# A third fast pair in the output projection, and T sums rounded and split in one instruction each

## The reference

```
h = x + token_mixing(rmsnorm(x, norm_mix), ...)      # 4 mixers, gates, merged @ w_out
h = h + peer_ffn(rmsnorm(h, norm_ffn), wq, subkeys, u, v)

# end of token_mixing
merged = sum over 4 branches of sigmoid(z @ gate_up[i]) * (o_i @ w_branch_i)
return merged @ w_out                                # 4096 x 4096: the output projection

# peer_ffn: queries, top-k keys, act = gelu(xn @ u.T), a sparse coefficient matrix, then
return wmat @ v                                      # 4096 x 4096: the last stage
```

## Time and profile before

| | us |
|---|---|
| median of three runs | 1894.08 |
| the profiled execution's own time | 1893.71 |
| its span, first to last instruction | 1891.9 |
| TensorE busy (8855 matmuls) | 1887.2 |
| VectorE busy | 1477.8 |
| ScalarE busy | 979.1 |
| GpSimd busy | 72.1 |

### The profile page before, as it was taken

The page is one execution under the profiler, slowest core; times in us unless marked ns, Lnnn a source line. Parts: engine busy times, 40 slices in busy tenths (PEclk is TensorE's granted clock), DMA queues, the critical chain, the costliest instruction groups (busy, mean ns, idle before and its releaser), DMA issues.

```text
span 1891.9 us, 25741 instructions
## 1 busy us (share of the span) xinstructions
PE 1887.2 (100%) x8855; PEld 1560.3 (82%) x8855; DVE 1477.8 (78%) x2159; ACT 979.1 (52%) x1195; POOL 72.1 (4%) x109
## 2 busy tenths in 40 slices
PE   9999999999999999999999999999999999999999
PEld 8888878888888888888888888888888888888887
DVE  7578875685567889989765555899989978999897
ACT  7654644445466556546454464444444455555553
POOL 0010020210100000000000000000000000000000
PEclk9999999999999999999999999999999999999999
DMA  9976667767675569867887776767766678666664
GB/s 325 349 226 167 184 196 239 202 179 237 204 235 173 183 196 298 270 227 235 260 262 225 218 224 220 232 206 222 220 202 200 200 210 291 222 215 220 213 221 156
DMA packets 202384, 423.96 MB, mean 224 GB/s; under 512 B 46752, under 2 KB 125216, under 8 KB 201504
## 3 DMA queue, kind: packets, MB, share of 16 engines
q1 hardware_dynamic: 174048, 369.35, 62.9%
q0 software_dynamic: 7248, 27.92, 4.3%
q10 hardware_dynamic: 20976, 25.19, 3.9%
HBM read 395.79 MB, written 26.61 MB: 223 GB/s over the span
## 4 chain that ended last, share of the span: by engine, by line
PE 100%; DMA 0%; ACT 0%; DVE 0%; SPq 0%; issue 0%
PE acc L707 26%; PE acc L710 25%; PE acc L714 25%; PE acc L755 3%; PE acc L757 3%; PE acc L761 3%; PE acc L1193 2%; PE side L1072 1%; PE side L1071 1%; PE side L1073 1%; PE acc L1199 1%; PE acc L1113 1%; PE acc L1112 1%; PE acc L1118 1%; PE side L882 1%; PE side L999 1%
## 5 line engine op out<-in xcount | busy, mean ns | idle before, releaser
L1660 DVE TENSOR_TENSOR w_lo<-w_raw,w_hi 128x1024 fp32r<-128x1024 f32 (+1 forms) x649 | 784.9, 1213 | 367.6 <-ACT w_hi L1240 361.0
L1240 ACT ACTIVATE w_hi<-w_raw 128x1024 fp32r<-128x1024 f32 (+1 forms) x649 | 680.7, 1052 | 722.7 <-PE acc L714 585.7
L707 PE MATMUL acc<-w_hi,xt_hi 128*128 128x512 f32 x1348 | 366.4, 394 | 0.0
L710 PE MATMUL acc<-w_hi,xt_lo 128*128 128x512 f32 x1348 | 360.6, 389 | 0.0
L714 PE MATMUL acc<-w_lo,xt_hi 128*128 128x512 f32 x1348 | 360.5, 389 | 0.0
L710 PEld LDWEIGHTS acc<-w_hi,xt_lo 128*128 128x128 f32 x1348 | 253.1, 188 | 53.0
L707 PEld LDWEIGHTS acc<-w_hi,xt_hi 128*128 128x128 f32 x1348 | 251.3, 188 | 55.2 <-issue 4.9
L714 PEld LDWEIGHTS acc<-w_lo,xt_hi 128*128 128x128 f32 x1348 | 253.1, 188 | 52.8
L707 PE MATMUL acc<-w_hi,x_hi 128*128 128x512 f32 x640 | 173.5, 393 | 0.0
L710 PE MATMUL acc<-w_hi,x_lo 128*128 128x512 f32 x640 | 171.3, 390 | 0.0
L714 PE MATMUL acc<-w_lo,x_hi 128*128 128x512 f32 x640 | 171.2, 390 | 0.0
(11 more groups left out here) (387 smaller groups left out, 2076.0 us busy)
## 6 DMA issues: line engine op xcount, KB each, us to landing
w_raw<-in_stream SPq DMA_DIRECT2D x504, 512.0 KB, 4.2
w_raw<-in_w_in SPq DMA_DIRECT2D x16, 496.0 KB, 3.9
w_raw<-in_w_in SPq DMA_DIRECT2D x16, 480.0 KB, 5.2
w_raw<-in_w_in SPq DMA_DIRECT2D x16, 464.0 KB, 4.0
w_raw<-in_w_in SPq DMA_DIRECT2D x16, 448.0 KB, 4.2
w_raw<-in_w_in SPq DMA_DIRECT2D x16, 432.0 KB, 3.9
w_raw<-in_w_in SPq DMA_DIRECT2D x16, 416.0 KB, 4.6
w_raw<-in_w_in SPq DMA_DIRECT2D x16, 400.0 KB, 3.7
```

The costliest lines, as they stand in the source:

```text
L707: pe.matmul(o[h], lhs(k0 + j, h)[0], wh[j], start=first and j == 0, stop=False)
L710: pe.matmul(o[h], lhs(k0 + j, h)[1], wh[j], start=False, stop=False)
L1240: nc.scalar.activation(w_hi[:, slot, 0:width], w_raw[:, slot, 0:width], ACT.Copy).then_inc(hi_ready, 1)
L1660: nc.vector.tensor_tensor(w_lo[:, slot, 0:width], w_raw[:, slot, 0:width], w_hi[:, slot, 0:width].bitcast(F32), ALU.subtract).then_inc(lo_ ...
```

## The change

A third pair is put in the output projection, groups 4 and 5, with six fast k pairs (`FAST`); two plain groups are left. Pairs of the last stage are renumbered from 3. The T sums of a fast k pair are rounded by one ScalarE instruction of 2048 columns and split by one VectorE instruction of 2048 columns; TensorE waits for both halves ahead of its first T matmul. The third pair adds its side banks at the times of the long pairs (`late`) and has its own `out_sums`. The row work of groups 2 to 5 starts 14, 12, 16 and 8 chunks later. The loads of x for groups 4 and 5 wait until the last T of the output projection is used, those for groups 6 and 7 until the third pair's side banks are added; `h_hi` waits for the last T too, from group 2 on.

```diff
@@ -106,11 +106,12 @@
-OUT_PAIRS = (Pair(0, CH_OUT, FAST[4:], 0), Pair(1, CH_OUT + 2 * CPG, FAST, 2))
-V_PAIRS = (Pair(2, CH_V, FAST_LAST[5:], 8), Pair(3, CH_F, FAST_LAST, 10), Pair(4, CH_F + 2 * CPG, FAST_LAST, 17),
-           Pair(5, CH_F + 4 * CPG, FAST_LAST, 24))
-OUT_PLAIN = CH_OUT + 4 * CPG
-HEAD = {0: 2, 2: 4}
+OUT_PAIRS = (Pair(0, CH_OUT, FAST[4:], 0), Pair(1, CH_OUT + 2 * CPG, FAST, 2), Pair(2, CH_OUT + 4 * CPG, FAST, 8))
+OUT_T = 14
+V_PAIRS = (Pair(3, CH_V, FAST_LAST[5:], OUT_T), Pair(4, CH_F, FAST_LAST, 16), Pair(5, CH_F + 2 * CPG, FAST_LAST, 23),
+           Pair(6, CH_F + 4 * CPG, FAST_LAST, 30))
+OUT_PLAIN = CH_OUT + 6 * CPG
+HEAD = {0: 2, 3: 4}
@@ -417,7 +418,8 @@
     out_t_lo = at("out_t_lo", [P, 2, 2, 512], F32R, PJ0 + 8 * KB)
-    out_sums = [at(f"out_sums{i}", [P, 512], F32, MG0 + (8 + 2 * i) * KB) for i in range(2)]
+    out_sums = [[at(f"out_sums{n}{i}", [P, 512], F32, MG0 + (8 + 4 * (n // 2) + 2 * i) * KB) for i in range(2)]
+                for n in range(len(OUT_PAIRS))]
     t_tiles = {True: (out_t_raw, out_t_hi, out_t_lo), False: (t_raw, t_hi, t_lo)}
@@ -575,13 +577,13 @@
     GATE_OUT = {MIX_CH[b] + n * (1 + MIX_K[b] // 2) + LEAD: (b, n) for b in MERGE for n in range(GRP)}
-    OUT_OUT = {CH_OUT + (n + 1) * CPG + LEAD: n for n in range(4, GRP)}
+    OUT_OUT = {CH_OUT + (n + 1) * CPG + LEAD: n for n in range(6, GRP)}
     MIX_HI = {mix_end("a", n) + LEAD + 8: n for n in range(GRP)}
-    ROW_END = {n: CH_OUT + {0: 2 * CPG, 1: 2 * CPG + 20, 2: 4 * CPG, 3: 4 * CPG + 10}.get(n, (n + 1) * CPG)
+    ROW_END = {n: CH_OUT + {0: 2 * CPG, 1: 2 * CPG + 20, 2: 4 * CPG + 14, 3: 4 * CPG + 22, 4: 6 * CPG, 5: 6 * CPG + 8}.get(n, (n + 1) * CPG)
                for n in range(GRP)}
@@ -1077,8 +1079,8 @@
-                if pair.order > 2:
-                    pe.wait_ge(block_free, 4 * (pair.order - 3) + 2 * i + h + 1)
+                if pair.order > 3:
+                    pe.wait_ge(block_free, 4 * (pair.order - 4) + 2 * i + h + 1)
                 elif h == 0:
@@ -1093,9 +1095,9 @@
                     for d in range(2):
-                        pe.wait_ge(t_hi_done, 2 * n + d + 1)
-                        pe.wait_ge(t_lo_done, 2 * n + d + 1)
                         if d == 0:
+                            pe.wait_ge(t_hi_done, 2 * n + 2)
+                            pe.wait_ge(t_lo_done, 2 * n + 2)
                             thrice(side[:, 1, :], s_tile[0], t, 0, first, last)
@@ -1121,14 +1123,14 @@
                     pe.wait_ge(xt_lo_done, KT + kp + 1)
-                if pair.order == 2:
+                if pair.order == 3:
                     pe.wait_ge(wmat_lo, kp + 1)
-                if first and pair.order in (1, 3, 4, 5):
+                if first and pair.order in (1, 2, 4, 5, 6):
                     pe.wait_ge(pure_free, pair.order)
-                if first and pair.order == 2:
+                if first and pair.order == 3:
                     pe.wait_ge(gates_put, ROUNDS)
                 if first:
-                    pe.wait_ge(s_lo_done, 12 if pair.order >= 2 else 8)
+                    pe.wait_ge(s_lo_done, 12 if pair.order >= 3 else 8)
                 def to_c21():
...
@@ -1402,6 +1404,8 @@
                 act.wait_ge(row_moved, 16 * (n + 1))
+                if n >= 2:
+                    act.wait_ge(t_used, OUT_T)
                 if k >= NX2:
@@ -1599,9 +1603,9 @@
                     act.wait_ge(t_used, n)
-                for d in range(2):
-                    act.wait_ge(t_made, 2 * n + d + 1)
-                    nc.scalar.activation(flat(hi_tile[:, d]), flat(raw[:, d]), ACT.Copy).then_inc(t_hi_done, 1)
+                act.wait_ge(t_made, 2 * n + 2)
+                nc.scalar.activation(hi_tile[:].rearrange("p d j n -> p (d j n)"),
+                                     raw[:].rearrange("p d j n -> p (d j n)"), ACT.Copy).then_inc(t_hi_done, 2)
@@ -2352,9 +2356,9 @@
                     dve.wait_ge(t_lo_done, 2 * n)
-                if kp == pair.fast[0] and pair.order == 2:
+                if kp == pair.fast[0] and pair.order == 3:
                     dve.wait_ge(s_lo_done, 12)
-                if kp == pair.fast[0] and pair.order in (1, 3, 4, 5):
+                if kp == pair.fast[0] and pair.order in (1, 2, 4, 5, 6):
                     dve.wait_ge(pure_free, pair.order)
@@ -2370,10 +2374,9 @@
                 raw, hi_tile, lo_tile = t_tiles[pair in OUT_PAIRS]
-                for d in range(2):
-                    dve.wait_ge(t_hi_done, 2 * n + d + 1)
-                    nc.vector.tensor_tensor(flat(lo_tile[:, d]), flat(raw[:, d]), flat(hi_tile[:, d]).bitcast(F32),
-                                            ALU.subtract).then_inc(t_lo_done, 1)
+                dve.wait_ge(t_hi_done, 2 * n + 2)
+                low, raws, hi = (t[:].rearrange("p d j n -> p (d j n)") for t in (lo_tile, raw, hi_tile))
+                nc.vector.tensor_tensor(low, raws, hi.bitcast(F32), ALU.subtract).then_inc(t_lo_done, 2)
@@ -2386,16 +2389,16 @@
                     return rows[:, h, n * 512:(n + 1) * 512]
-                n = 2 * (pair.order - 2) + i
+                n = 2 * (pair.order - 3) + i
                 return h_rows[:, h, n * 512:(n + 1) * 512]
-                u, v = (t[:] for t in (out_sums if pair in OUT_PAIRS else sums))
+                u, v = (t[:] for t in (out_sums[pair.order] if pair in OUT_PAIRS else sums))
                 p1, p5, p6, p7 = (side[:, i, :] for i in range(4))
                     dve.wait_ge(t_used, pair.first_t + len(pair.fast))
-                    if pair.order == 2:
+                    if pair.order == 3:
                         dve.wait_ge(h_loaded, 64)
@@ -2438,7 +2441,8 @@
-                if pair.fast[-1] == 12:
+                late = pair.fast[-1] == 12 or pair.order == 2
+                if late:
                     for step, at in enumerate(((14, 1), (14, 1), (15, 0), (15, 1))):
@@ -2447,7 +2451,7 @@
                         t_sums(after, 0)
-                if kp in (13, 14) and pair.fast[-1] < 12:
+                if kp in (13, 14) and not late:
                     add_pure(pair, 2 * (kp - 13) + i)
@@ -2475,12 +2479,12 @@
                 if pair:
-                    pair_tasks(pair, kp, i, {0: OUT_PAIRS[1], 2: V_PAIRS[1]}.get(pair.order))
+                    pair_tasks(pair, kp, i, {0: OUT_PAIRS[1], 1: OUT_PAIRS[2], 3: V_PAIRS[1]}.get(pair.order))
                 between(s)
             for pair in V_PAIRS[1:]:
-                before = V_PAIRS[pair.order - 3]
-                after = V_PAIRS[pair.order - 1] if pair.order < 5 else None
+                before = V_PAIRS[pair.order - 4]
+                after = V_PAIRS[pair.order - 2] if pair.order < 6 else None
                 for kp in range(CPG):
@@ -2602,7 +2606,9 @@
                 if n == 4:
-                    pool.wait_ge(pure_free, 2)
+                    pool.wait_ge(t_used, OUT_T)
+                if n == 6:
+                    pool.wait_ge(pure_free, 3)
                 pool.dma_start(rows[:, :, n * 512:(n + 1) * 512], io["x"][:, :, n * 512:(n + 1) * 512])\
```

More of the change, by code:

```diff
@@ L516, in group_number @@
     def group_number(pair, i):
-        return GN_OUT + 2 * pair.order + i if pair in OUT_PAIRS else GN_V + 2 * (pair.order - 2) + i
+        return GN_OUT + 2 * pair.order + i if pair in OUT_PAIRS else GN_V + 2 * (pair.order - 3) + i
     def pair_bank(pair, i):
```

## The result

The changed kernel takes 1897.61 us (median of 20 runs, 1895.49 to 1900.47); the kernel before, run beside it on the same chip, 1894.26 us (20 runs, 1893.52 to 1896.23). The ratio is 1.0017, with a 95% interval of 1.0011 to 1.0023: 3.35 us slower, where the forecast of 1894.1 us meant no change to speak of, and 0.8 us outside the range. The profiled execution took 1897.63 us with a span of 1895.9 us, 4.0 us more than before; the granted clock is at its higher level throughout (1.000).

The account below looks back on a forecast made before the run. TensorE was taken as the bound, number of matmuls times pitch. 1893.71 (profiled execution) - 4.08 + 2.93 (existing fast k pairs' stalls) + 1.18 (third pair's) = 1893.74 us; the median stands 0.37 higher, 1894.1 us; 8 in 10 from 1891.8 to 1896.8.

Parts of the forecast that it names:

- The third pair's 4.08 us: Output projection: six fast k pairs drop 18 matmuls at 0.2267 us, 4.08 us off TensorE.
- Moved row work: Groups 2 to 5, moved later, cost nothing, covered by VectorE's 1.49 us idle per plain chunk; 13 us without cover.
- The durations: The new 2048-column instructions: ScalarE's rounding taken as 1.90 us, VectorE's split as 2.29 us.
- The hand-over: Passing T from one engine to the next, taken as 0.03 us; up to 0.1 us in range for TensorE's wake-up.
- The openings: Opening of a pair in the last stage, three times: TensorE stalls 0.53 us each, 1.59 us together.
- The third pair's own stalls: Output projection: 0.33 us for a bank at the opening and 0.85 us at k pair 2, sum 1.18 us.
- Second pair, k pair 8: Output projection: rounding starts 0.26 us later and TensorE stalls 0.76 us for the merged T.
- the first pair's k pair 8: Output projection: the merged T comes after TensorE's load at 804.03 us, a stall of 0.58 us.
- k pairs 0, 2, 4 and 10 keep 0.6 us or more: Second pair of the output projection: these k pairs keep 0.6 us or more to spare, so no stall.
- (a): Rival: the full gain, TensorE finds every T ready, 1890.0 us; chance 0.09.
- (b): Rival: only the three openings and the first pair stall, the third pair runs through, 1892.2 us; chance 0.25.
- (c): Rival: slower, VectorE's period and weight-ring refills bound the third pair, 10.9 us against 10.2, giving 1898.5 us; chance 0.06.

Follow-up runs that it names:

- e10: The changed kernel with the row work of group 0 put six chunks later: 1895.71 us, ratio 1.0010 to the kernel before.
- e1: The kernel before, without the third pair, with T rounded and split in single 2048-column instructions and TensorE waiting for both halves: 1899.71 us, ratio 1.0029.
- e4: The changed kernel with T still rounded in one 2048-column instruction, but split in two of 1024 and waited for by halves: 1891.10 us, ratio 0.9981.
- e3: The changed kernel with T rounded and split in two instructions each, TensorE still waiting for both halves: 1892.36 us, ratio 0.9989.

## Why the prediction was wrong, step by step

- *The third pair's 4.08 us*: right; alone it gives 4.3 us in the medians and 4.0 in the spans. *Moved row work: nothing*: right too, for groups 2 to 5 (the third pair alone has no wait). The group that did cost was one that was not moved, group 0.
- *The durations* 1.90 and 2.29 us: measured 1.92 and 2.29. The Trainium skill's rule ("VectorE: DVE Perf Modes", TRN2 errata) gives 2.291 us for 2048 columns. The trace agrees, with 2.292. The saving per fast k pair against two of 1024 is (54.1 + 33.0) / 37 - (52.7 + 32.1) / 37 = 0.06 us, as worked out from the rows (the first two numbers are VectorE's busy time in the same groups of the third pair alone). On the path it is worth nothing.
- *The hand-over*: 0.03 us is what the trace of before shows from ScalarE to VectorE, but merged it is 0.10 us there, 0.11 from VectorE to ScalarE and 0.11 on to TensorE's load. That the need still came out near the 7.0 measured (the forecast's terms make 6.96) is partly luck: three hand-overs make it 0.24 us longer, and the matmul that starts 0.03 us behind its load, not 0.22, takes 0.2 back.
- *The openings*, 3 x 0.53: mechanism right, measured 0.58 and the restart, 0.70 each, 2.1 us for 1.59. The restart, 0.09 to 0.14 us a stop, is in no term of the forecast.
- *The third pair's own stalls*, 0.33 + 0.85: right in place; 0.29 and 0.92 with two restarts, 1.4 for 1.18. (The sum of VectorE's period there is 9.2 us, not 9.1; it changes nothing.)
- *Second pair, k pair 8*: 0.88 and the restart, 1.0 for 0.76.
- **First failed step: the first pair's k pair 8, 0.58 us.** The lead was taken as 6.4 us from one execution and held fixed. It measured 5.4, the stall 1.59 and the restart, and ahead of it, in the same pair, stand the 0.27 us and a restart at 788.71: 2.1 for 0.58, the largest miss. Halves need only 5.5 us, so the trace of before had no stall to show that this place was loose. Why the lead fell is open, as said above.
- **Second failed step: "k pairs 0, 2, 4 and 10 keep 0.6 us or more".** At k pair 4 the later end of T's split pushes the transpose, the DMA issue behind it on ScalarE's queue and the next rounding: 1.3 us of lead gone, a stall of 0.48 and the restart, 0.57 us where nothing was forecast. I had listed what stands behind the merged instructions on their own engines, priced at nothing by ScalarE's idle time, and not followed it to the wait on the other queue. Experiment e10 shows it.
- *The cost of merging alone* was forecast at 2.93 us and is 5.3 (e1).
- *The rivals*: (a) and (b) fell with the count of stalls; (c), slower by refills in the third pair, named the right side and nearly the time (1898.5), but by luck, for a reason that is wrong: no refill wait bounds the third pair, and without merging it runs through.

Summed: 2.1 + 0.57 + 1.0 + 1.4 + 2.1 = 7.2 us of stalls and restarts in the profile of after, against 4.11 us forecast.

## What to carry to other kernels

Joining the halves of a tile that three engines pass on saved VectorE 0.06 us of busy time a tile here and turned a pipeline (need 5.5 us) into a chain (7.0 us); do it only where the lead measured in several executions exceeds the chain. Ask of every consumer how long before its use the chain starts, and count what a late instruction holds up on the other engines' queues, not only on its own. A place without a stall in one profile tells nothing of its margin: margins that hang on transfers differed here by 1.5 us (first pair) and 3.7 us (first pair of the last stage) between the profiled executions of twelve kernels.

## What the runs showed of the hardware

A stop of TensorE costs more than its own length: in the profile of after the matmul that had waited is followed by the next one after 0.31 us instead of 0.227 at all seven T stalls (0.48 to 1.59 us long), and within ten matmuls each of these stops has cost 0.09 to 0.13 us more.

A hand-over in the serial line took 0.11 us from VectorE to ScalarE (1640.47 to 1640.58), 0.10 us back (1642.50 to 1642.61 in the rounded rows, 0.10 at all 37 merged splits) and 0.11 us from VectorE to TensorE's weight load (1644.90 to 1645.01). Before a split of 1024 columns the hand-over from ScalarE to VectorE is 0.03 us (840.78 to 840.81 in the kernel before, and e4, where only the rounding is merged); why it differs by the length of the instruction that waits, no run shows.

The 2048-column copy on ScalarE takes 1.92 us; the halves of e3 add up to 2.07 us a tile (76.5 us of ScalarE's busy time over 37), so merging saves ScalarE 0.15 us, more than twice VectorE's 0.06.
